# Transposed probabilities copied a pair at a time, out of two banks by one instruction

## The chip, the cores and the metric

The kernel runs on one core of one Trainium2 chip. The metric is the device time of one execution in microseconds (us), the median of three runs. A profiled execution gives the trace: which engine ran what, when, and what ended each idle stretch.

The engines by the names of the profile: PE multiplies matrices (PEld is its weight load), DVE is the vector engine, ACT the scalar engine, POOL the general one, SP issues transfers. Each runs its own instructions in order, and they wait for one another by semaphores. PE writes into PSUM, eight banks of 512 fp32 columns on 128 partitions; ACT and DVE read it.

## What is computed

Two encoder trunks with the same weights, one over 512 tokens (s = 0) and one over 1024 (s = 1), two layers each. A layer projects its input, runs three kinds of attention side by side, gates them, projects back and normalises:

```python
def encoder_layer(x, ...):
    h = x @ w_in
    (a_q, a_k, a_v, a_g, b_cq, b_ckv, b_kr, b_g, c_q, c_k, c_v, c_g) = jnp.split(h, split_at, axis=-1)
    oa = window_attn(a_q, a_k, a_v, sink, t5_table) * jax.nn.silu(a_g)       # 8 heads, +-128 tokens
    ob = mla(b_cq, b_ckv, b_kr, ...) * jax.nn.silu(b_g)                      # 4 heads, all tokens
    oc = neighborhood_attn(c_q, c_k, c_v, rpb) * jax.nn.silu(c_g)            # 4 heads, 2-D window
    o = jnp.concatenate([oa, ob, oc], axis=-1) @ w_out
    return layer_norm(DEEPNORM_ALPHA * x + o, ln_g, ln_b)
```

Each attention is scores, softmax, and probabilities times values.

## The kernel before

**Stages.** Within a layer, first s = 0 and then s = 1: input projections, attention A (windowed), C (neighbourhood), B (all positions), output projection, normalisation. PE takes most of its time for the projections (`products`, L564), which the change leaves alone.

**Units, pairs and halves.** Attention is cut into units of 128 queries by one head. A and C units see two or three tiles of 128 keys (256 or 384 columns); B units see all, four tiles for s = 0 and eight for s = 1. Two units that follow one another are a pair. The probabilities of a unit are transposed by PE in halves of at most four key tiles, so a B unit of s = 1 has two halves (hf 0 and 1) and every other unit one. Per layer there are, in pairs, 16 in A, 8 in C and 8 in B for s = 0, and 32, 16 and 16 for s = 1.

**One unit's way.** PE computes scores into PSUM (`score`). DVE reduces them to a bound and, in A and C, adds the bias on the way into `pAC` (`bound_scores`, L1027, L1038, L1044). ACT takes the exponential (`exp_unit`, L813 and L817). PE transposes the probabilities into bank 4 or bank 5 (`transpose_probs`, L661). One of ACT and DVE copies the bank into `pt_sb` (`pt_copy`, L824 on ACT and L1052 on DVE). PE multiplies by the values (`values`, L693), and after every second pair transposes the reciprocal sums (L699).

**Who copies.** `copied_by_act` numbers all halves and gives the even ones to ACT and the odd ones to DVE. Both units of a pair are transposed one behind the other into banks 4 and 5, so ACT copies the first unit's bank and DVE the second's, side by side.

**What sets the order.** PE's order is `pe_steps`. In A and C cycle j is: scores of pair j, transposes of pair j-1, values of pair j-2. In B cycle j is: scores of unit 2j, transposes of pair j-1, scores of unit 2j+1, for s = 1 the transposes of the second half, values of pair j-1. ACT and DVE walk over units: at step i, DVE does the bound of unit i, then its copy of unit i-2; every fourth step it adds `group_scale` (L1072), `group_rinv` (L1058) and `group_out` (L1078). ACT at step i does its copy of unit i-2, then the exponential of unit i. In B of s = 1, steps 2j and 2j+1 hold the copies of half 0 and half 1 of pair j-1.

**What PE waits for.** A transpose waits for the probabilities and for the copy of what stood in its bank two halves earlier; the values wait for the copies of their half. Both go through `wait_copied`. The copies go to four slots of `pt_sb`, so two pairs of halves are held at once.

Of the kernel before, what the change touches and what calls it, by code (L numbers as in the profile page):

```python
# [21 lines left out]
ACT = mybir.ActivationFunctionType  # L22
AX = mybir.AxisListType

P = 128
# [91 lines left out]
def units_of(phase, s):  # L117
    return {"A": a_units, "C": c_units, "B": b_units}[phase](s)
# [11 lines left out]
def halves_of(u, s):  # L130

    n = key_tiles(u, s)
    return [range(c, min(c + 4, n)) for c in range(0, n, 4)]
# [61 lines left out]
LAG_T, LAG_FIN = 2, 6  # L195
# [5 lines left out]
def encoder_kernel(nc, ins, y_out):  # L201
# [18 lines left out]
    with ctx:  # L220
# [128 lines left out]
        def halves(s, ph):  # L349
            return halves_in_order(ph, s)  # L350


        half_index = {}
# [4 lines left out]
            unit_index.update({(s, x): n % STAT_COLS for n, x in enumerate(x for ph in "ACB" for x in units_of(ph, s))})  # L358

        def copied_by_act(s, u, hf):  # L360
            return half_index[s, (u, hf)] % 2 == 0

        all_units = [(s, u) for s in range(2) for ph in "ACB" for u in units_of(ph, s)]
        all_groups = [(s, ph, g) for s in range(2) for ph in "ACB" for g in range(len(units_of(ph, s)) // 4)]
# [41 lines left out]

        probs_no = Numbered(all_units)
        score_no = probs_no
        pt_act_no = Numbered([(s, h) for s in range(2) for ph in "ACB" for h in halves(s, ph) if copied_by_act(s, *h)])
        pt_dve_no = Numbered([(s, h) for s in range(2) for ph in "ACB" for h in halves(s, ph) if not copied_by_act(s, *h)])  # L410
        group_no = Numbered(all_groups)
        xh_no = Numbered([("xT", s, t, i) for s in range(2) for t in range(NTILES[s]) for i in range(2)])
        split_no = Numbered([(s, u) for s in range(2) for u in UNITS])
# [40 lines left out]
        def wait_full(eng, key):  # L454
            b, n, _ = uses[key]
            eng.wait_ge(bank_full[b], n + 1)
            return bank[b]
# [97 lines left out]
        def _(pe):  # L555
# [87 lines left out]
                last.then_inc(full(("fill", s, ph)), 1)  # L643

            def wait_copied(s, half):
                if copied_by_act(s, *half):
                    pe.wait_ge(pt_act, pt_act_no[s, half])
                else:
                    pe.wait_ge(pt_dve, pt_dve_no[s, half])

            def transpose_probs(s, ph, j, hf):
                for i in (2 * j, 2 * j + 1):
# [22 lines left out]
            def values(s, ph, j):  # L675


                okey = ("O", s, ph, j // 2)
                b = uses[okey][0]
                if j % 2 == 0:  # L680
                    wait_free(pe, okey)
                    if j == 2 and ph in FILLERS:
                        wait_full(pe, ("fill", s, ph))
                pair = units_of(ph, s)[2 * j:2 * j + 2]
                nk = key_tiles(pair[0], s)
                cols = slice(P * (j % 2), P * (j % 2) + P)
                for hf, chunks in enumerate(halves_of(pair[0], s)):
                    for u in pair:
                        wait_copied(s, (u, hf))
                    for c in chunks:  # L690
                        for k, u in enumerate(pair):
                            slot = half_index[s, (u, hf)] % 4
                            nc.tensor.matmul(bank[b][64 * k:64 * k + 64, cols], value_tile(s, u, c),  # L693
                                             pt_sb[:, slot, (c % 4) * P:(c % 4 + 1) * P], start=(c == 0), stop=(c == nk - 1))
                if j % 2:
                    g = j // 2
                    pe.wait_ge(rinv_spread, group_no[s, ph, g])
                    for m in range(2):
                        last = nc.tensor.transpose(bank[b][:, 256 + P * m:256 + P * m + P], rinv_wide[:, P * m:P * m + P], ident[:, :])  # L699
                    last.then_inc(bank_full[b], 1)  # L700
# [62 lines left out]
        def _(act):  # L763
# [53 lines left out]
                    nc.scalar.activation(pAC[:, i % 3, 0:m], pAC[:, i % 3, 0:m], ACT.Exp, bias=nmax[:, j:j + 1],  # L817
                                         scale=-1.0, accum_out=psums[:, j:j + 1]).then_inc(probs_done, 1)

            def pt_copy(s, u, hf):  # L820
                if copied_by_act(s, u, hf):
                    ps = wait_full(act, ("PT", s, u, hf))
                    n = len(halves_of(u, s)[hf]) * P
                    nc.scalar.activation(pt_sb[:, half_index[s, (u, hf)] % 4, 0:n], ps[:, 0:n], ACT.Copy).then_inc(pt_act, 1)  # L824

            layer_ln = (ln_stat, ln_sqrt, ln_coef, ln_norm)

# [6 lines left out]
            with act.Fori(0, DEPTH) as layer:  # L834
# [16 lines left out]
                for s, NT in enumerate(NTILES):  # L851
# [50 lines left out]
                    for ph in "ACB":  # L902
# [26 lines left out]
                        for i in range(len(U) + LAG_T):  # L929
                            if 0 <= i - LAG_T < len(U):  # L930
                                if ph == "B" and s:
                                    for u in U[i // 2 * 2 - 2:i // 2 * 2]:
                                        pt_copy(s, u, i % 2)
                                else:
                                    pt_copy(s, U[i - LAG_T], 0)
                            if i < len(U):
                                exp_unit(s, i, U[i])
                    for g in range(2):
# [14 lines left out]
        def _(dve):  # L953
# [91 lines left out]
                                                   scale=1.0, scalar=3e38, op0=ALU.add, op1=ALU.min,  # L1045
                                                   accum_out=nmax[:, j:j + 1]).then_inc(score_done, 1)

            def pt_copy(s, u, hf):
                if not copied_by_act(s, u, hf):
                    ps = wait_full(dve, ("PT", s, u, hf))  # L1050
                    n = len(halves_of(u, s)[hf]) * P
                    nc.vector.tensor_copy(pt_sb[:, half_index[s, (u, hf)] % 4, 0:n], ps[:, 0:n]).then_inc(pt_dve, 1)  # L1052

            def group_rinv(s, ph, g):
                u = units_of(ph, s)[4 * g + 3]
# [31 lines left out]
            with dve.Fori(0, DEPTH) as layer:  # L1087
                for s, NT in enumerate(NTILES):
# [61 lines left out]
                    for ph in "ACB":  # L1150
# [31 lines left out]
                        for i in range(len(U) + LAG_FIN):  # L1182
                            if i < len(U):
                                bound_scores(s, i, U[i])
                            if 0 <= i - LAG_T < len(U):
                                if ph == "B" and s:
                                    for u in U[i // 2 * 2 - 2:i // 2 * 2]:
                                        pt_copy(s, u, i % 2)
                                else:
                                    pt_copy(s, U[i - LAG_T], 0)  # L1190
                            if i >= 5 and (i - 5) % 4 == 0 and i - 5 < len(U):
                                group_rinv(s, ph, (i - 5) // 4)
                            if i >= 8 and (i - 8) % 4 == 0 and i - 8 < len(U):
# [393 lines left out]
```

## Time and profile before

| | |
|---|---|
| three runs | 2022.31 us median (2020.79 to 2022.73) |
| the profiled execution | 2022.05 us, its span 2020.2 us |
| PE busy, share of the span | 1844.7 us, 91% |
| DVE busy | 961.1 us, 48% |
| ACT busy | 788.1 us, 39% |
| copies into `pt_sb` on ACT (L824) | 224, 113.2 us |
| copies into `pt_sb` on DVE (L1052) | 224, 127.2 us |
| PE's part of the chain that ended last | 85% |

The busy shares are means over stages with different limits. In the first layer the stages that copy are, in us from the span's start: A of s = 0 at 195 to 234, C at 234 to 252, B at 274 to 315; for s = 1, A at 640 to 720, C at 720 to 763, B at 808 to 917. The second layer repeats them.

In the rows a line of the timeline is: start in us, length in us, engine, line, operation, output and inputs, shapes, count, and in brackets the idle time before it with the event that ended it. A new instruction on DVE or ACT may start about 0.1 us before the one ahead of it is shown to end.

### The profile page before, as it was taken

How to read it: one execution, taken by the hardware profiler on the slowest of the kernel's cores; microseconds unless marked ns; L12 is line 12 of the kernel's file. 1: busy time of each engine (PE TensorE's matmuls, PEld its weight loads, DVE VectorE, ACT ScalarE, POOL GpSimd, SP SyncE). 2: the span in 40 equal slices, each digit the busy share in tenths (PEclk: the TensorE clock that was granted, in tenths of full speed). 3: DMA queues.
4: the chain of work that ended last, by engine and by line, in shares of the span. 5: the costliest groups of instructions: out<-in, count | busy, mean ns of one | idle time of the engine just before them, and what ended most of it. 6: DMA issues, size and time to landing. Idle time of an engine off the chain costs nothing.

```text
span 2020.2 us, 32850 instructions
## 1 busy us (share of the span) xinstructions
PE 1844.7 (91%) x12594; PEld 1491.3 (74%) x12594; DVE 961.1 (48%) x2226; ACT 788.1 (39%) x1651; POOL 423.8 (21%) x484
## 2 busy tenths in 40 slices
PE   1899978999999998999959999789999999989996
PEld 0697657889987665888948865588898866568796
DVE  7334744511423875554441466443124267555626
ACT  3323643322123665552222356332112256645512
POOL 4322211311110063001132213023010102600003
PEclk9899999999999999999979999999999999999998
DMA  7464305211124110005035450332112251000312
GB/s 256 134 198 127 95 1 199 86 55 47 53 73 118 40 60 0 1 1 188 32 122 157 138 157 12 141 100 67 59 43 59 68 136 34 27 1 2 136 53 84
DMA packets 149023, 169.76 MB, mean 84 GB/s; under 512 B 18384, under 2 KB 134736, under 8 KB 148352
## 3 DMA queue, kind: packets, MB, share of 16 engines
q1 hardware_dynamic: 146928, 161.24, 25.9%
q10 hardware_dynamic: 1504, 4.78, 0.6%
q8 instruction: 104, 1.70, 0.3%
q0 software_dynamic: 432, 1.57, 0.2%
q14 instruction: 55, 0.45, 0.1%
HBM read 145.49 MB, written 32.65 MB: 88 GB/s over the span
## 4 chain that ended last, share of the span: by engine, by line
PE 85%; DVE 8%; ACT 3%; issue 2%; POOL 1%; DMA 1%; SPq 0%; ACTq 0%; DVEq 0%; POOLq 0%
PE psum L564 62%; PE psum L693 8%; PE psum L661 7%; PE psum L635 5%; DVE nmax L1027 2%; PE psum L699 2%; DVE pt_sb L1052 1%; DVE gT L976 1%; DVE x_lo L1018 1%; ACT pAC L817 1%; DVE qB_lo L1179 0%; POOL w_lo L451 0%; DMA qkC<-ln_in_b 0%; PE psum L642 0%; PE psum L573 0%
## 5 line engine op out<-in xcount | busy, mean ns | idle before, releaser
L564 PE MATMUL psum<-w_hi,x_hi 128*128 128x256 f32 x1344 | 383.9, 286 | 21.7 <-DVE x_lo L1199 14.1
L564 PE MATMUL psum<-w_lo,x_hi 128*128 128x256 f32 x1344 | 383.1, 285 | 0.0
L564 PE MATMUL psum<-w_hi,x_lo 128*128 128x256 f32 x1344 | 382.8, 285 | 0.0
L564 PE MATMUL psum<-x_hi,w_hi 128*128 128x512 f32 x816 | 324.3, 397 | 10.7 <-DVE x_lo L1018 10.7
L564 PE MATMUL psum<-x_hi,w_lo 128*128 128x512 f32 x816 | 324.8, 398 | 0.0
L564 PE MATMUL psum<-x_lo,w_hi 128*128 128x512 f32 x816 | 324.1, 397 | 0.0
L451 POOL TENSOR_TENSOR w_lo<-w_stage,w_hi 128x1024 fp32r<-128x1024 f32 (+1 forms) x82 | 162.3, 1989 | 731.4 <-ACT w_hi L848 731.3
L451 DVE TENSOR_TENSOR w_lo<-w_stage,w_hi 128x1024 fp32r<-128x1024 f32 (+1 forms) x78 | 138.9, 1797 | 331.8 <-ACT w_hi L848 331.8
L564 PEld LDWEIGHTS psum<-w_hi,x_hi 128*128 128x128 f32 x1344 | 259.5, 193 | 23.4 <-issue 23.2
L564 PEld LDWEIGHTS psum<-w_lo,x_hi 128*128 128x128 f32 x1344 | 259.6, 193 | 0.2
L564 PEld LDWEIGHTS psum<-w_hi,x_lo 128*128 128x128 f32 x1344 | 259.6, 193 | 0.0
L848 ACT ACTIVATE w_hi<-w_stage 128x1024 fp32r<-128x1024 f32 (+1 forms) x160 | 129.0, 859 | 243.0 <-PE psum L564 194.0
L824 ACT ACTIVATE pt_sb<-psum 128x256 f32<-128x256 f32 (+2 forms) x224 | 113.2, 505 | 218.1 <-PE psum L661 216.8
L564 PEld LDWEIGHTS psum<-x_hi,w_hi 128*128 128x128 f32 x816 | 154.4, 189 | 48.2 <-issue 11.1
L564 PEld LDWEIGHTS psum<-x_lo,w_hi 128*128 128x128 f32 x816 | 154.5, 189 | 37.7
L564 PEld LDWEIGHTS psum<-x_hi,w_lo 128*128 128x128 f32 x816 | 154.3, 189 | 37.1
L1274 POOL COPY rinv_wide<-rinv 128x256 f32<-128x256 f32 x96 | 38.3, 399 | 662.1 <-DVE rinv L1058 662.1
L817 ACT ACTIVATE pAC<-pAC,nmax 128x385 f32<-128x385 f32 (+3 forms) x288 | 164.8, 574 | 22.3 <-DVE nmax L1044 12.2
L1027 DVE TENSOR_REDUCE nmax<-psum 128x1 f32<-128x1024 f32 (+1 forms) x96 | 100.5, 1047 | 142.7 <-PE psum L564 141.4
L661 PEld LDWEIGHTS psum<-ident,pAC 128*128 128x128 f32 x768 | 81.4, 141 | 72.8 <-ACT pAC L817 63.5
L1052 DVE COPY pt_sb<-psum 128x256 f32<-128x256 f32 (+2 forms) x224 | 127.2, 568 | 11.7 <-PE psum L661 11.6
L1038 DVE CUSTOM_DVE_ANT_0 pAC<-psum,biasA,nsink 128x384 f32<-128x384 f32 (+1 forms) x192 | 108.6, 568 | 46.2 <-PE psum L635 41.0
(146 smaller groups left out, 2680.0 us busy)
## 6 DMA issues: line engine op xcount, KB each, us to landing
w_stage<-w_in SPq DMA_DIRECT2D x48, 512.0 KB, 4.4
w_stage<-w_in SPq DMA_DIRECT2D x88, 256.0 KB, 3.2
toep<-rpb_tile SPq DMA_DIRECT2D x12, 1152.0 KB, 15.4
rpb_tile<-rpb_col SPq DMA_DIRECT2D x48, 192.0 KB
qA<-y SPq DMA_DIRECT2D x18, 512.0 KB, 5.2
hT<-y SPq DMA_DIRECT2D x18, 512.0 KB, 11.2
y<-hT SPq DMA_DIRECT2D x18, 512.0 KB, 2.6
w_stage<-w_out SPq DMA_DIRECT2D x32, 256.0 KB, 4.0
```

Of the source, the lines that this page charges most:

```text
L451: last = eng.tensor_tensor(lo, src, hi.bitcast(F32), ALU.subtract)
L564: last = nc.tensor.matmul(out, w, x, start=(n == 0), stop=(n == len(pairs) - 1))
L635: nc.tensor.matmul(ps[:, 0:n], w, x, start=True, stop=True).then_inc(full(("S", s, u, 0)), 1)
L661: last = nc.tensor.transpose(ps[:, (c % 4) * P:(c % 4 + 1) * P], src[:, c * P:(c + 1) * P], ident[:, :])
L693: nc.tensor.matmul(bank[b][64 * k:64 * k + 64, cols], value_tile(s, u, c), pt_sb[:, slot, (c % 4) * P:(c % 4 + 1) * P], start=(c == 0), st ...
L699: last = nc.tensor.transpose(bank[b][:, 256 + P * m:256 + P * m + P], rinv_wide[:, P * m:P * m + P], ident[:, :])
L817: nc.scalar.activation(pAC[:, i % 3, 0:m], pAC[:, i % 3, 0:m], ACT.Exp, bias=nmax[:, j:j + 1], scale=-1.0, accum_out=psums[:, j:j + 1]).th ...
L824: nc.scalar.activation(pt_sb[:, half_index[s, (u, hf)] % 4, 0:n], ps[:, 0:n], ACT.Copy).then_inc(pt_act, 1)
L848: last = nc.scalar.activation(hi, src, ACT.Copy)
L1027: nc.vector.tensor_reduce(nmax[:, j:j + 1], b_scores(s, i), AX.XY, ALU.min).then_inc(score_done, 1)
L1038: nc.vector.tensor_tensor_reduce(out=pAC[:, i % 3, 0:n], in0=ps[:, 0:n], in1=reversed_keys(biasA[:, t - 1, kv, :] if t else biasA0[:, kv, ...
L1052: nc.vector.tensor_copy(pt_sb[:, half_index[s, (u, hf)] % 4, 0:n], ps[:, 0:n]).then_inc(pt_dve, 1)
```

## The change

A pair of halves is copied by one instruction that reads banks 4 and 5 together and writes two neighbouring slots of `pt_sb`. One engine copies the whole pair: ACT the even pairs, DVE the odd ones. The semaphores `pt_act` and `pt_dve` count pairs instead of halves, and `wait_copied` waits for the pair that a half belongs to. In A, C and B of s = 0 both engines have the copy at odd steps only, on DVE behind the bound and on ACT ahead of the exponential; in B of s = 1 half 0 of every pair falls to ACT and half 1 to DVE.

```diff
         def copied_by_act(s, u, hf):
-            return half_index[s, (u, hf)] % 2 == 0
+            return half_index[s, (u, hf)] // 2 % 2 == 0
...
             def wait_copied(s, half):
-                if copied_by_act(s, *half):
-                    pe.wait_ge(pt_act, pt_act_no[s, half])
+                first = half_list[s][half_index[s, half] // 2 * 2]
+                if copied_by_act(s, *first):
+                    pe.wait_ge(pt_act, pt_act_no[s, first])
                 else:
-                    pe.wait_ge(pt_dve, pt_dve_no[s, half])
+                    pe.wait_ge(pt_dve, pt_dve_no[s, first])
...
                 for hf, chunks in enumerate(halves_of(pair[0], s)):
-                    for u in pair:
-                        wait_copied(s, (u, hf))
+                    wait_copied(s, (pair[0], hf))
...
-            def pt_copy(s, u, hf):
-                if not copied_by_act(s, u, hf):
-                    ps = wait_full(dve, ("PT", s, u, hf))
-                    n = len(halves_of(u, s)[hf]) * P
-                    nc.vector.tensor_copy(pt_sb[:, half_index[s, (u, hf)] % 4, 0:n], ps[:, 0:n]).then_inc(pt_dve, 1)
+            def pair_copy(s, ph, j, hf):
+                pair = units_of(ph, s)[2 * j:2 * j + 2]
+                if not copied_by_act(s, pair[0], hf):
+                    for u in pair:
+                        wait_full(dve, ("PT", s, u, hf))
+                    n = len(halves_of(pair[0], s)[hf]) * P
+                    slot = half_index[s, (pair[0], hf)] % 4
+                    nc.vector.tensor_copy(pt_sb[:, slot:slot + 2, 0:n], psum[:, 4:6, 0:n]).then_inc(pt_dve, 1)
...
                                 if ph == "B" and s:
-                                    for u in U[i // 2 * 2 - 2:i // 2 * 2]:
-                                        pt_copy(s, u, i % 2)
-                                else:
-                                    pt_copy(s, U[i - LAG_T], 0)
+                                    pair_copy(s, ph, i // 2 - 1, i % 2)
+                                elif i % 2:
+                                    pair_copy(s, ph, i // 2 - 1, 0)
```

ACT's `pt_copy` becomes a `pair_copy` in the same way, with `nc.scalar.activation(..., ACT.Copy)`.

DVE in attention B of s = 1, in the kernel before: the bound of a unit is `nmax<-psum`, a copy is `pt_sb<-psum`.

```order
L1027 TENSOR_REDUCE nmax<-psum 128x1
L1052 COPY pt_sb<-psum 128x512
L1027 TENSOR_REDUCE nmax<-psum 128x1
L1052 COPY pt_sb<-psum 128x512
L1027 TENSOR_REDUCE nmax<-psum 128x1
L1052 COPY pt_sb<-psum 128x512
L1072 TENSOR_TENSOR gT<-psum,gT 128x2x128
L1027 TENSOR_REDUCE nmax<-psum 128x1
L1052 COPY pt_sb<-psum 128x512
L1058 RECIPROCAL rinv<-psums 128x4
```

DVE at the same place in the changed kernel.

```order
L1030 TENSOR_REDUCE nmax<-psum 128x1 x2
L1058 COPY pt_sb<-psum 128x1024
L1030 TENSOR_REDUCE nmax<-psum 128x1
L1078 TENSOR_TENSOR gT<-psum,gT 128x2x128
L1030 TENSOR_REDUCE nmax<-psum 128x1
L1058 COPY pt_sb<-psum 128x1024
L1064 RECIPROCAL rinv<-psums 128x4
```

One copy of 1024 columns stands behind every second bound, where one of 512 stood behind each.

DVE in attention A of s = 1, before, the steps of two units with `group_scale` and `group_out` among them; a bound is the three rows that begin with `pAC,nmax<-psum`.

```order
L1038 ISA pAC,nmax<-psum,biasA,nsink 128x384
L1038 ISA nmax 128x1
L1041 COPY pAC<-nsink 128x1
L1072 TENSOR_TENSOR gT<-psum,gT 128x256
L1038 ISA pAC,nmax<-psum,biasA,nsink 128x384
L1038 ISA nmax 128x1
L1041 COPY pAC<-nsink 128x1
L1052 COPY pt_sb<-psum 128x384
L1058 RECIPROCAL rinv<-psums 128x4
L1078 TENSOR_TENSOR gT<-psum,gT 128x256
```

DVE at the same steps in the changed kernel.

```order
L1041 ISA pAC,nmax<-psum,biasA,nsink 128x384
L1041 ISA nmax 128x1
L1044 COPY pAC<-nsink 128x1
L1078 TENSOR_TENSOR gT<-psum,gT 128x256
L1041 ISA pAC,nmax<-psum,biasA,nsink 128x384
L1041 ISA nmax 128x1
L1044 COPY pAC<-nsink 128x1
L1058 COPY pt_sb<-psum 128x2x384
L1064 RECIPROCAL rinv<-psums 128x4
L1084 TENSOR_TENSOR gT<-psum,gT 128x256
```

The copy keeps its place between the second bound and the reciprocal, and now covers both banks; the next two bounds have no copy behind them, since ACT takes that pair.

## Rows read from the trace of the kernel before

**Rows 1.** The chain that ended last, by line: 640 to 662, then 823 to 834 us.

```profile
by line: PE psum L661 27.2%; PE psum L693 26.8%; PE psum L635 25.0%; PE psum L642 9.0%; ACT pAC L817 5.5%; PE psum L699 5.0%; ACT pt_sb L824 1.7%; issue 0.3%
...
by line: PE psum L564 35.7%; DVE nmax L1027 22.3%; PE psum L693 19.9%; DVE pt_sb L1052 11.1%; PE psum L661 8.0%; issue 3.8%; DVEq L456 0.4%
```

**Rows 2.** Windows: stretch, length, busy us per engine, PE clock, DMA share, GB/s.

```profile
640.00:719.60 79.60, 79.55 (x696) 51.17 (x696) 63.05 (x270) 53.37 (x160) 6.90 (x17) 1.00 0.33 90
...
808.00:917.30 109.30, 106.35 (x952) 88.01 (x950) 60.63 (x84) 55.03 (x92) 3.20 (x8) 1.00 0.07 24
...
281.00:311.70 30.70, 21.86 (x189) 17.08 (x187) 13.75 (x26) 12.26 (x30) 1.20 (x3) 1.00 0.05 13
```

**Rows 3.** Groups by shape, whole span: count, busy us, mean ns, idle before.

```profile
L1027 DVE TENSOR_REDUCE nmax<-psum 128x1 f32<-128x1024 f32 x64 | 78.4, 1224 | 99.4 <-PE psum L564 98.2
...
L1052 DVE COPY pt_sb<-psum 128x512 f32<-128x512 f32 x80 | 54.5, 681 | 9.5 <-PE psum L661 9.5
...
L1052 DVE COPY pt_sb<-psum 128x384 f32<-128x384 f32 x96 | 52.7, 549 | 1.1 <-PE psum L661 1.1
...
L824 ACT ACTIVATE pt_sb<-psum 128x512 f32<-128x512 f32 x80 | 47.8, 597 | 121.5 <-PE psum L661 121.5
...
L824 ACT ACTIVATE pt_sb<-psum 128x384 f32<-128x384 f32 x96 | 47.1, 490 | 65.8 <-PE psum L661 64.8
```

**Rows 4.** Timeline, B of s = 1: one cycle, then the last pair.

```profile
823.92 1.23 DVE L1027 TENSOR_REDUCE nmax<-psum 128x1 f32<-128x1024 f32 x1 [0.44 <-PE psum L564]
...
825.06 0.68 DVE L1052 COPY pt_sb<-psum 128x512 f32<-128x512 f32 x1
...
825.89 1.09 PE L693 MATMUL psum<-pt_sb,vB 128*64 128x128 f32 x16 [0.17 <-DVE pt_sb L1052]
...
913.58 0.69 DVE L1052 COPY pt_sb<-psum 128x512 f32<-128x512 f32 x1 [2.30 <-PE psum L661]
...
913.89 1.16 PE L661 MATMUL psum<-ident,pB 128*128 128x128 f32 x8 [0.34 <-ACT pt_sb L824]
...
915.09 0.69 DVE L1052 COPY pt_sb<-psum 128x512 f32<-128x512 f32 x1 [0.48 <-PE psum L661]
```

**Rows 5.** Timeline, B of s = 0: one cycle, an even pair.

```profile
287.18 0.69 DVE L1027 TENSOR_REDUCE nmax<-psum 128x1 f32<-128x512 f32 x1 [2.26 <-PE psum L564]
...
288.74 0.69 DVE L1027 TENSOR_REDUCE nmax<-psum 128x1 f32<-128x512 f32 x1 [0.87 <-PE psum L564]
289.35 0.68 DVE L1052 COPY pt_sb<-psum 128x512 f32<-128x512 f32 x1
289.47 0.69 ACT L813 ACTIVATE pB<-psum,nmax 128x512 f32<-128x512 f32 x1 [0.59 <-DVE nmax L1027]
...
290.18 1.09 PE L693 MATMUL psum<-pt_sb,vB 128*64 128x128 f32 x16 [1.47 <-DVE pt_sb L1052]
```

**Rows 6.** Timeline, A and C of s = 1: DVE's copy and PE's next transposes.

```profile
650.18 0.55 DVE L1052 COPY pt_sb<-psum 128x384 f32<-128x384 f32 x1
...
650.99 0.87 PE L661 MATMUL psum<-ident,pAC 128*128 128x128 f32 x6
...
655.46 0.55 DVE L1052 COPY pt_sb<-psum 128x384 f32<-128x384 f32 x1
...
656.06 0.88 PE L661 MATMUL psum<-ident,pAC 128*128 128x128 f32 x6
...
741.20 0.55 DVE L1052 COPY pt_sb<-psum 128x384 f32<-128x384 f32 x1
...
742.27 0.87 PE L661 MATMUL psum<-ident,pAC 128*128 128x128 f32 x6
```

**Rows 7.** Timeline, A of s = 0: DVE's copy and PE's next transposes.

```profile
220.13 0.54 DVE L1052 COPY pt_sb<-psum 128x384 f32<-128x384 f32 x1
...
220.52 1.04 PE L661 MATMUL psum<-ident,pAC 128*128 128x128 f32 x6
...
221.01 0.31 PEld L661 LDWEIGHTS psum<-ident,pAC 128*128 128x128 f32 x3 [0.18 <-ACT pAC L817]
```

More of the change, by code:

```diff
@@ L408, in encoder_kernel @@
         score_no = probs_no
-        pt_act_no = Numbered([(s, h) for s in range(2) for ph in "ACB" for h in halves(s, ph) if copied_by_act(s, *h)])
-        pt_dve_no = Numbered([(s, h) for s in range(2) for ph in "ACB" for h in halves(s, ph) if not copied_by_act(s, *h)])
+        pt_act_no = Numbered([(s, h) for s in range(2) for ph in "ACB" for h in halves(s, ph)[::2] if copied_by_act(s, *h)])
+        pt_dve_no = Numbered([(s, h) for s in range(2) for ph in "ACB" for h in halves(s, ph)[::2] if not copied_by_act(s, *h)])
         group_no = Numbered(all_groups)
@@ L818, in exp_unit @@
                                          scale=-1.0, accum_out=psums[:, j:j + 1]).then_inc(probs_done, 1)
-            def pt_copy(s, u, hf):
-                if copied_by_act(s, u, hf):
-                    ps = wait_full(act, ("PT", s, u, hf))
-                    n = len(halves_of(u, s)[hf]) * P
-                    nc.scalar.activation(pt_sb[:, half_index[s, (u, hf)] % 4, 0:n], ps[:, 0:n], ACT.Copy).then_inc(pt_act, 1)
+            def pair_copy(s, ph, j, hf):
+                pair = units_of(ph, s)[2 * j:2 * j + 2]
+                if copied_by_act(s, pair[0], hf):
+                    for u in pair:
+                        wait_full(act, ("PT", s, u, hf))
+                    n = len(halves_of(pair[0], s)[hf]) * P
+                    slot = half_index[s, (pair[0], hf)] % 4
+                    nc.scalar.activation(pt_sb[:, slot:slot + 2, 0:n], psum[:, 4:6, 0:n], ACT.Copy).then_inc(pt_act, 1)
             layer_ln = (ln_stat, ln_sqrt, ln_coef, ln_norm)
@@ L1046, in bound_scores, with pair_copy @@
                                                    accum_out=nmax[:, j:j + 1]).then_inc(score_done, 1)
-            def pt_copy(s, u, hf):
-                if not copied_by_act(s, u, hf):
-                    ps = wait_full(dve, ("PT", s, u, hf))
-                    n = len(halves_of(u, s)[hf]) * P
-                    nc.vector.tensor_copy(pt_sb[:, half_index[s, (u, hf)] % 4, 0:n], ps[:, 0:n]).then_inc(pt_dve, 1)
+            def pair_copy(s, ph, j, hf):
+                pair = units_of(ph, s)[2 * j:2 * j + 2]
+                if not copied_by_act(s, pair[0], hf):
+                    for u in pair:
+                        wait_full(dve, ("PT", s, u, hf))
+                    n = len(halves_of(pair[0], s)[hf]) * P
+                    slot = half_index[s, (pair[0], hf)] % 4
+                    nc.vector.tensor_copy(pt_sb[:, slot:slot + 2, 0:n], psum[:, 4:6, 0:n]).then_inc(pt_dve, 1)
             def group_rinv(s, ph, g):
@@ L1186, in _ @@
                                 if ph == "B" and s:
[L1187 to L1190, printed above, removed]
+                                    pair_copy(s, ph, i // 2 - 1, i % 2)
+                                elif i % 2:
+                                    pair_copy(s, ph, i // 2 - 1, 0)
                             if i >= 5 and (i - 5) % 4 == 0 and i - 5 < len(U):
```

## The prediction

> **What bounds the kernel now.** I read the chain of work that ended last first, cut to the stages that copy, since the change touches nothing else. In A of s = 1 it is PE's lines one after another: scores, transposes, values and reciprocal transposes make 93% of that stretch, and the 7% of ACT lie at the stage's start [rows 1]. PE is busy for 79.55 of 79.60 us there, DVE for 63.05 and ACT for 53.37 [rows 2]. So A is PE's own pace, and time that DVE or ACT saves is worth nothing unless PE waits for it. In B of s = 1 the same view is another picture: DVE's bound has 22.3% of the chain and DVE's copy 11.1% [rows 1]. The timeline shows how. The scores of the second unit end, DVE's bound starts at 823.92, DVE's copy follows at 825.06, and PE's second half of the values starts at 825.89 after 0.17 us of waiting for that copy [rows 4]. In B of s = 0 the wait is 1.47 us in each pair, on the same two DVE steps: bound at 288.74, copy at 289.35, values at 290.18 [rows 5]. What counts is therefore when the last copy of a pair ends, and not how much copying there is.
>
> **What a pair copy costs.** The trace has no copy out of two banks. It has copies of 384 and 512 columns: 549 and 681 ns on DVE, 490 and 597 ns on ACT [rows 3]. That is 132 and 107 ns for each 128 columns, with about 153 and 169 ns that do not depend on size. Carried on, 768 columns take 0.945 us on DVE and 0.811 on ACT, and 1024 columns 1.209 and 1.025. A reduction over two banks exists, 1024 columns in 1.224 us [rows 3], which speaks for DVE's figure. From below, two banks could be read at once, which would make it 0.68; from above, crossing into a second bank could cost the fixed part again, 0.15 more. I take the slope. From the end of a copy to the PE work that waits for it I take 0.15 us: 825.06 + 0.68 to 825.89 [rows 4].
>
> So one instruction replaces two, and saves 0.15 us of engine time for each pair. But the two ran side by side on two engines, and now one engine does both: the pair is ready 0.53 us later on DVE (1.209 for 0.681), or 0.40 with A's shapes (0.945 for 0.549). The page "Advanced Engine Details and Errata" of the Trainium skill, section "The Read-Write Bubble", advises large tiles and one instruction over several banks, since latency shows between instructions; by it the saved 0.15 us would be the whole effect. The rows agree that there is such a fixed part, and say that it lies on an engine that has time to spare. The page "Perfetto Trace Analysis" of the same skill, section "Optimizing Scalar/DVE Operations", grants grouping its gain only on a saturated engine, and otherwise advises splitting where the engine holds up another; this stage is of the second kind.
>
> **B of s = 1.** ACT's copy of half 0 takes 0.43 us longer than the one it had; the transposes of half 1 that wait for it may slip by a tenth or so, and that lies under the later wait. Half 1 is now all DVE's and stands behind the second unit's bound, as DVE's single copy did. It starts at 825.06 and ends 1.209 later, so the second half of the values starts at 826.42 in place of 825.89 [rows 4]: 0.53 us for each pair that has scores beside it. There are 15 such pairs a layer, 30 in all: **15.9 us**. The last pair has no scores to fill the time. ACT's pair copy starts when both units are transposed, at 913.58, and ends with the 0.15 at 914.76; PE's transposes of half 1, now at 913.89, wait for it, 0.87 more [rows 4]. They push DVE's copy from 915.09 to 915.96, and that takes 0.53 longer, part of which lies under the first half of the values: 1.3 us together, for two layers **2.6 us**.
>
> **B of s = 0.** There is a sign each way. Even pairs go to ACT, whose order is now exponential, pair copy, exponential. The bound starts at 287.18, the exponential follows it by 0.73 (288.74 to 289.47) and takes 0.69, the pair copy ends 1.025 + 0.15 later at 289.78, against 290.18 now [rows 5]: 0.40 gained, since this copy is no longer behind the second unit's bound. Odd pairs go to DVE behind that bound and lose 0.53. Four of each per layer: 0.5 us a layer, **1.0 us**.
>
> **A of s = 1.** DVE now has its pair copy in every second cycle, the one in which it also has `group_scale`, the reciprocal and `group_out`. PE's next transposes need bank 4 first, and the wait for it is now for the whole pair; before, that was ACT's early copy. DVE's copy starts at 650.18 and would end with the 0.15 at 651.27, where PE starts at 650.99: 0.28 lost. Where a pair of two key tiles lies next to it PE is sooner: copy from 655.46 to 656.56, PE at 656.06, 0.50 lost [rows 6]. In eight pairs (one head group over eight query tiles) there are two of the latter, one of the former and one, where the copied pair itself is of two tiles, with none: 1.28 us. Four head groups and two layers: **10.2 us**. Behind the pair copy the next bounds start up to 0.4 late. The exponentials that follow are due a whole cycle later, so I take nothing. In the other cycles ACT's pair copy stands ahead of the second exponential, 0.32 us longer than ACT's copy now. Worked through with the durations above, the transposes that wait for this exponential have 0.1 to 0.2 us left, so I take nothing; if all 72 ACT pairs of A and C lost the whole 0.32 it would be 23 us.
>
> **A of s = 0.** Every fourth pair loses: copy from 220.13, ready at 221.22, PE due at 220.52, 0.70 lost. A wait of 0.18 for the second unit's exponential stands there already [rows 7] and goes under, so 0.52 remains, four times a layer: **4.2 us**.
>
> **C.** The bound is shorter and the copy comes earlier against PE: ready at 742.30 for a start at 742.27 [rows 6], 0.03. POOL's bias rows hang on the reciprocal, which comes 0.40 later; I find them still in time. Ten such places a layer at 0.03 to 0.15: **1.5 us**.
>
> **The ends of A and C.** There the transposes of the last pair have no scores ahead of them and nothing but the previous values to cover them, and ACT's longer copy before the last exponential shows too. No row gives it. It lies between 0.28 (the ordinary stall) and 1.3 (the end of B); I take 0.65, for eight ends **5.2 us**.
>
> **Sum.** 15.9 + 2.6 + 1.0 + 10.2 + 4.2 + 1.5 + 5.2 = 40.6 us on the profiled execution's 2022.05 (0.26 below the median of the runs): **2063 us**, 2.0% slower. Projections, loads and output stages stand as they were, and everything after an attention stage waits for it, so I see no place that gives a stall back.
>
> **The rivals.** *Only B counts* (12%). The profile books PE's idle before the transposes of A to ACT's exponential, as at 221.01 [rows 7]. If PE waits for that anyway, the later copy hides in A, C and their ends, and 19.5 us remain: 2042. Against it is PE's busy time of 79.55 in 79.60 [rows 2].
>
> *The clock falls* (4%). PE's waits could bring it from 2.4 to 1.2 GHz in a stage. If B of s = 0 fell in both layers, its 21.9 us of PE work [rows 2] would double, 44 us more: 2107. Against it: in that stretch PE is busy for 21.86 of 30.70 us and the granted clock is 1.00 all the same [rows 2], and no stage becomes emptier than that.
>
> *DVE's time is what paces* (3%), the case on the faster side. Were the loop in A and C closed over DVE's queue, each of the 112 DVE pairs would give back 0.153 us: 17 us, 2005. It decides from the point where DVE has no idle time left; DVE has 63.05 of 79.60 [rows 2]. The skill's "Perfetto Trace Analysis" puts DVE's cost per instruction on PSUM at about 125 ns, by which the estimate would be 14 us and 2008; no run here shows that it is on PE's way.
>
> *Two banks are read at once* (2%). A pair copy would last as long as one bank's copy does. Then B of s = 1 and A lose little and the even pairs of B of s = 0 gain 0.8 each: about 2020, no change to speak of. Against it is the reduction, which takes 1.224 us for two banks.
>
> **How the numbers follow.** My forecast has 79%. Its own range is 2048 to 2080: below, the smaller ends and A's stalls in part; above, 0.15 more per pair copy at some 90 places (13 us) or a part of ACT's 23 us. To hold 8 in 10 the low end goes to 2040, which takes in the case of B alone: **2040 to 2080**. A measurement of this kernel tells changes of over 0.2% from none. Faster by that: 3%. Within: 2%. Slower: 95%.
>
> **What would show it.** In the profile after: 112 copies each on ACT and DVE, DVE's of 1024 columns near 1.21 us and of 2x384 near 0.95. PE idle of about 0.7 us before the second half of the values in B of s = 1, released by DVE's copy, and B of s = 1 about 9 us longer. PE idle of 0.3 to 0.7 before every second group of transposes in A, released by DVE's copy, and A of s = 1 some 5 to 6 us longer. In B of s = 0 waits that alternate, shorter after ACT's copy and longer after DVE's. It would be wrong if the pair copies came out shorter than the slope says, if A stayed at 79.6 us, or if idle time showed up before transposes and belonged to ACT's exponential.

## The result, and the profile after

| | before | after |
|---|---|---|
| median, us (runs) | 2022.52 (2020.79 to 2023.47) | 2057.77 (2052.62 to 2061.85) |
| ratio, 95% interval | | 1.0174 (1.0145 to 1.0203) |
| profiled execution, span | 2022.05, 2020.2 | 2054.34, 2052.5 |
| B of s = 1, layers 1 and 2 | 151.86, 152.66 | 159.94, 159.92 |
| B of s = 0 | 60.79, 59.23 | 61.03, 61.04 |
| A of s = 1 | 81.59, 81.58 | 86.55, 86.55 |
| A of s = 0 | 38.95, 38.96 | 41.71, 41.70 |
| C of s = 1 | 43.06, 43.07 | 44.25, 44.26 |
| C of s = 0 | 17.37, 17.36 | 18.29, 18.29 |

The kernel became 1.7% slower. A stage length runs from PE's first instruction of the stage, for B its own projections included, to the end of its last values. Together the stages of both layers are 37.0 us longer; the rest of the profiled execution is 4.8 us shorter, though the change touches nothing there. The clock, of which the last section tells, moves single stages by 1 to 4 us from one execution to another.

The page after, first its engines: all three that the change touches are busy for a smaller share, in a longer span.

```profile
PE 1851.2 (90%) x12594; PEld 1487.8 (72%) x12594; DVE 952.9 (46%) x2114; ACT 774.8 (38%) x1539; POOL 424.4 (21%) x484
```

First two groups of the kernel before, the values of B and the transposes of A and C, with count, busy us, mean ns and idle before:

```profile
L693 PE MATMUL psum<-pt_sb,vB 128*64 128x128 f32 x1280 | 87.3, 278 | 27.6 <-DVE pt_sb L1052 27.6
...
L661 PE MATMUL psum<-ident,pAC 128*128 128x128 f32 x768 | 119.1, 284 | 4.6 <-ACT pAC L817 4.0
```

The groups of the kernel after. L1058 and L828 are the pair copies on DVE and ACT, L694 the values, L663 the transposes.

```profile
L694 PE MATMUL psum<-pt_sb,vB 128*64 128x128 f32 x1280 | 87.9, 279 | 37.6 <-DVE pt_sb L1058 32.0 <-ACT pt_sb L828 5.5
...
L663 PE MATMUL psum<-ident,pAC 128*128 128x128 f32 x768 | 117.8, 282 | 18.2 <-DVE pt_sb L1058 11.4 <-ACT pAC L818 3.3 <-ACT pt_sb L828 2.6
...
L1058 DVE COPY pt_sb<-psum 128x1024 f32<-128x1024 f32 x40 | 48.6, 1216 | 12.9 <-PE psum L663 12.9
L1058 DVE COPY pt_sb<-psum 128x768 f32<-128x768 f32 x48 | 45.7, 951 | 2.0 <-PE psum L663 2.0
...
L828 ACT ACTIVATE pt_sb<-psum 128x1024 f32<-128x1024 f32 x40 | 41.0, 1024 | 110.2 <-PE psum L663 110.2
...
L828 ACT ACTIVATE pt_sb<-psum 128x768 f32<-128x768 f32 x48 | 38.0, 791 | 0.0
```

A copy out of two banks costs what the slope of [rows 3] said: 1.216 and 0.951 us on DVE, 1.024 and 0.791 on ACT. And PE now waits for DVE's copy in two places: ahead of the values of B for 32.0 us, with 5.5 for ACT's beside it, where it was 27.6 in all, and ahead of the transposes for 11.4, where there was no such wait. All of the 11.4 us lie in A.

The chain that ended last, by line, in 11 us of B of s = 1 (834 to 845 us), answers to the second row of [rows 1]: DVE's copy has gone from 11.1% to 22.3%, the bound ahead of it from 22.3% to 16.1%.

```profile
by line: PE psum L564 29.5%; DVE pt_sb L1058 22.3%; PE psum L694 17.9%; DVE nmax L1030 16.1%; PE psum L663 7.9%; issue 6.7%; DVEq L456 0.4%
```

The timeline of the same cycle, then the last pair of the stage, beside [rows 4]:

```profile
834.32 1.23 DVE L1030 TENSOR_REDUCE nmax<-psum 128x1 f32<-128x1024 f32 x1 [1.06 <-PE psum L564]
...
835.47 1.22 DVE L1058 COPY pt_sb<-psum 128x1024 f32<-128x1024 f32 x1
...
836.73 1.09 PE L694 MATMUL psum<-pt_sb,vB 128*64 128x128 f32 x16 [0.57 <-DVE pt_sb L1058]
...
929.89 1.02 ACT L828 ACTIVATE pt_sb<-psum 128x1024 f32<-128x1024 f32 x1 [2.16 <-PE psum L663]
931.06 1.06 PE L663 MATMUL psum<-ident,pB 128*128 128x128 f32 x8 [1.26 <-ACT pt_sb L828]
...
933.51 1.09 PE L694 MATMUL psum<-pt_sb,vB 128*64 128x128 f32 x16 [0.36 <-DVE pt_sb L1058]
```

From the start of the bound to the second half of the values it was 1.97 us (823.92 to 825.89); now it is 2.41. Every cycle grew by as much, 7.02 and 7.24 us to 7.47 and 7.67.

B of s = 0, an even pair and the odd one behind it, beside [rows 5]:

```profile
302.37 1.01 ACT L828 ACTIVATE pt_sb<-psum 128x1024 f32<-128x1024 f32 x1
...
303.53 1.09 PE L694 MATMUL psum<-pt_sb,vB 128*64 128x128 f32 x16 [1.04 <-ACT pt_sb L828]
...
307.73 1.22 DVE L1058 COPY pt_sb<-psum 128x1024 f32<-128x1024 f32 x1
...
309.00 1.09 PE L694 MATMUL psum<-pt_sb,vB 128*64 128x128 f32 x16 [1.92 <-DVE pt_sb L1058]
```

The wait of 1.47 us in every pair has become 1.04 and 1.92 in turn.

A of s = 0 and two places in A of s = 1, DVE's pair copy and the transposes that wait for it, beside [rows 7] and [rows 6]:

```profile
220.34 0.95 DVE L1058 COPY pt_sb<-psum 128x768 f32<-128x768 f32 x1
...
221.44 0.85 PE L663 MATMUL psum<-ident,pAC 128*128 128x128 f32 x6 [0.64 <-DVE pt_sb L1058]
...
653.49 0.95 DVE L1058 COPY pt_sb<-psum 128x768 f32<-128x768 f32 x1
...
654.59 0.85 PE L663 MATMUL psum<-ident,pAC 128*128 128x128 f32 x6 [0.21 <-DVE pt_sb L1058]
...
659.02 0.95 DVE L1058 COPY pt_sb<-psum 128x768 f32<-128x768 f32 x1
...
660.12 0.85 PE L663 MATMUL psum<-ident,pAC 128*128 128x128 f32 x6 [0.42 <-DVE pt_sb L1058]
```

### The profile page after: what moved, and what is told of

The parts are those of the page before. It is cut to its first block, busy times and chain, and to the rows that moved or that the text cites. A ratio compares the mean times of both kernels' runs of the same rounds, so it can differ in the third digit from the quotient of the medians.

```text
span 2052.5 us, 32718 instructions
## 1 busy us (share of the span) xinstructions
PE 1851.2 (90%) x12594; PEld 1487.8 (72%) x12594; DVE 952.9 (46%) x2114; ACT 774.8 (38%) x1539; POOL 424.4 (21%) x484
## 4 chain that ended last, share of the span: by engine, by line
PE 79%; DVE 12%; ACT 4%; issue 3%; POOL 1%; DMA 1%; SPq 0%; ACTq 0%; DVEq 0%; POOLq 0%
PE psum L564 60%; PE psum L694 6%; PE psum L663 6%; DVE pt_sb L1058 4%; PE psum L635 4%; PE psum L700 2%; DVE nmax L1030 2%; DVE gT L979 1%; DVE pAC L1041 1%; ACT pt_sb L828 1%; DVE x_lo L1021 1%; ACT pAC L818 0%; DVE qB_lo L1185 0%; POOL w_lo L451 0%; DMA qkC<-ln_in_b 0%
## 5 line engine op out<-in xcount | busy, mean ns | idle before, releaser
L663 PEld LDWEIGHTS psum<-ident,pAC 128*128 128x128 f32 x768 | 81.2, 141 | 89.5 <-ACT pAC L818 65.6
L828 ACT ACTIVATE pt_sb<-psum 128x512 f32<-128x512 f32 (+2 forms) x112 | 92.9, 830 | 112.7 <-PE psum L663 112.5
L663 PE MATMUL psum<-ident,pAC 128*128 128x128 f32 x768 | 117.8, 282 | 18.2 <-DVE pt_sb L1058 11.4
## 6 DMA issues: line engine op xcount, KB each, us to landing
hT<-y SPq DMA_DIRECT2D x18, 512.0 KB, 11.4
```

What stands on the lines that cost most here:

```text
L663: last = nc.tensor.transpose(ps[:, (c % 4) * P:(c % 4 + 1) * P], src[:, c * P:(c + 1) * P], ident[:, :])
L828: nc.scalar.activation(pt_sb[:, slot:slot + 2, 0:n], psum[:, 4:6, 0:n], ACT.Copy).then_inc(pt_act, 1)
```

## Experiments

**Is it the merged instruction, or that one engine does both banks?** The kernel after, with each pair as two one-bank instructions on the same engine:

```diff
-                    nc.vector.tensor_copy(pt_sb[:, slot:slot + 2, 0:n], psum[:, 4:6, 0:n]).then_inc(pt_dve, 1)
+                    for k in range(2):
+                        last = nc.vector.tensor_copy(pt_sb[:, slot + k, 0:n], psum[:, 4 + k, 0:n])
+                    last.then_inc(pt_dve, 1)
```

and the same on ACT.

> The changed kernel, but each pair is copied by two instructions of one bank each on the pair's engine, with the signal on the second; engines, order and waits are those of the change. Theory (one engine now does both banks, so the pair's last copy ends late): the two run one behind the other and end about 0.06 us later than the one instruction (0.60 + 0.68 for 1.22), so B of s = 1 stays at 160 to 163 us a layer (152 before), A of s = 1 at 86.5 to 88 (81.6 before), and the time at 2055 to 2066. Rival (it is the instruction over two banks that costs, by itself or by meeting PE in the other bank): the time falls back to 2022 to 2030.

Measured: 2068.29 us (2066.87 to 2070.49), 1.0241 (1.0224 to 1.0258), a little above what was expected. The merge is no loss; without it the kernel is slower still. Of the 10.5 us between the two, 3.1 are not the copies': they lie ahead of the first values of B of s = 1 in the first layer, in a stretch whose granted clock is in the last section. A of s = 1 is 87.37 and 87.38. The timeline shows two DVE copies in a row, and the values behind them:

```profile
843.28 1.28 DVE L1061 COPY pt_sb<-psum 128x512 f32<-128x512 f32 x2
...
844.62 1.09 PE L694 MATMUL psum<-pt_sb,vB 128*64 128x128 f32 x16 [0.58 <-DVE pt_sb L1061]
```

Two copies take 1.28 us and one of twice the size 1.22. A merge thus saves 0.06 and not the 0.153 of the slope, because the second copy starts before the first is shown to end: each alone lasts 0.68.

**Is it DVE?** The kernel after, with all pair copies on ACT:

```diff
-            return half_index[s, (u, hf)] // 2 % 2 == 0
+            return True
```

> The changed kernel with every pair copy on ACT; DVE copies none. Theory: what counts is when the pair's copy ends, and on ACT it is not behind DVE's bound. B of s = 1 then goes back to about 152 us a layer, B of s = 0 gains 0.44 us in all eight pairs of a layer and falls to 56 or 57, A of s = 1 is between (82.5 to 85), because the pair copy now stands ahead of the second exponential in every cycle; the time is 2015 to 2032. Rival (ACT's longer copy ahead of the exponential is what cost the time): it stands there twice as often, so the time rises over 2058, and A of s = 1 over 87.

Measured: 2029.79 us (2026.14 to 2031.6), 1.005 (1.0033 to 1.0067), as the theory expected. Of the 35 us, 28 are gone with DVE's share of the copies, though ACT now does them all.

```profile
L694 PE MATMUL psum<-pt_sb,vB 128*64 128x128 f32 x1280 | 87.5, 279 | 20.4 <-ACT pt_sb L828 17.5
...
L663 PE MATMUL psum<-ident,pAC 128*128 128x128 f32 x768 | 124.5, 285 | 7.6 <-ACT pAC L818 3.3 <-ACT pt_sb L828 2.9
```

The values wait for 20.4 us, against 37.6 after and 27.6 before. B of s = 0 gains 4.5 us a layer on the kernel before (56.12 and 54.76), A of s = 1 still costs 2.9 (84.50). B of s = 1 has its ordinary cycles back (7.07 and 7.23 to 7.26), but not its 152 us: it takes 153.37 and 155.48, 1.1 of it more at the last pair and, in the second layer, 1.4 more ahead of its first values.

**How much of it is B of s = 1?** The kernel before, with the pair copies in that stage alone:

```diff
+        def merged(s, ph):
+            return s == 1 and ph == "B"
...
-            return half_index[s, (u, hf)] % 2 == 0
+            n = half_index[s, (u, hf)]
+            return n // 2 % 2 == 0 if merged(s, u[0]) else n % 2 == 0
```

> The kernel before with one part of the change alone: pair copies in B of s = 1, half 0 on ACT and half 1 on DVE; A, C and B of s = 0 copy by halves as before. Theory: the stages lose independently of one another, so B of s = 1 goes to about 160 us a layer and all other stages stay, 2036 to 2041. Rival (a general slowing, of the clock or of DMA, that shows in this stage): this stage alone gives much less, under 2030, or other stages move too.

Measured: 2039.74 us (2039.26 to 2040.1), 1.0097 (1.008 to 1.0113). The cycles are 7.49 and 7.67, as in the kernel after, and A and C stay as before to 0.01 us. That is 18.7 us over the runs of before beside it, about half of the 35, and B of s = 1 alone brings it. Not all of it is the copies': the stage takes 162.94 and 160.65 us, 19.1 more than in the trace of before, of which cycles and last pair make 16.0, and 3.1 lie ahead of the first layer's first values, at a mean granted clock of 0.86 where the kernel before had 0.96.

**Does the place behind the bound decide in B?** The kernel before, with DVE's copy ahead of the bound at B's odd steps:

```diff
+                            late = ph == "B" and i % 2
-                            if i < len(U):
+                            if i < len(U) and not late:
...
+                            if i < len(U) and late:
+                                bound_scores(s, i, U[i])
```

> The kernel before, copies by halves, with one thing moved: at odd steps of B DVE does its copy ahead of the bound instead of behind it. Theory (PE's values wait for the last copy, and it is late because it stands behind the bound of scores that PE has only just done): B of s = 0 loses its 1.47 us wait nearly whole, about 1.3 us in each of eight pairs, 59 to 49 us a layer; B of s = 1 loses its 0.2 us and goes to about 149; the time is 1993 to 2003. Rival (the bound, now later, holds up the exponential and with it the next transposes): waits move from the values to the transposes and the time stays within 2018 to 2030 or rises.

Measured: 2001.19 us (2000.62 to 2002.69), 0.9908 (0.9892 to 0.9925). In B of s = 0 the timeline has copy, then bound, and a wait of 0.18 in place of 1.47 [rows 5]:

```profile
292.32 0.69 DVE L1052 COPY pt_sb<-psum 128x512 f32<-128x512 f32 x1 [0.18 <-PE psum L661]
...
293.02 0.69 DVE L1027 TENSOR_REDUCE nmax<-psum 128x1 f32<-128x512 f32 x1
293.16 1.09 PE L693 MATMUL psum<-pt_sb,vB 128*64 128x128 f32 x16 [0.18 <-DVE pt_sb L1052]
```

B of s = 0 falls to 51.62 and 50.51 us, which shows the place as the cause of the wait. B of s = 1 does not fall to the 149 us of the theory (152.33 and 151.61). Only its cycles without a reciprocal gain (6.69); the others grow to 7.49, since the reciprocal stayed behind the bound and PE now waits for what POOL makes of it:

```profile
825.10 0.17 DVE L1058 RECIPROCAL rinv<-psums 128x4 f32<-128x4 f32 x1
...
825.79 0.44 PE L699 MATMUL psum<-ident,rinv_wide 128*128 128x128 f32 x2 [0.49 <-POOL rinv_wide L1277]
```

**The same in the changed kernel,** with pair copy and reciprocal ahead of the bound at B's odd steps (the diff as above, with the reciprocal moved too):

> The changed kernel with one thing moved: at odd steps of B, DVE's pair copy and the reciprocal stand ahead of the bound instead of behind it. Theory: the pair copy is late in B because of the bound it stands behind, and a copy over two banks is not dear in itself. B of s = 0 falls from 61 to about 55.5 us a layer (only the DVE pairs gain, 1.3 each), B of s = 1 from 160 to about 155.5 (the copy is then bound by its own 1.22 us behind the transposes), A and C stay; 2034 to 2042. Rival (one engine for both banks is what costs, wherever its copy stands): B of s = 1 stays near 160 and the time at 2050 or more.

Measured: 2047.55 us (2045.47 to 2048.74), 1.0129 (1.0112 to 1.0146): better than after by 10 us, and short of what was expected. B of s = 0 came near the forecast (56.26, 56.15 for 55.5), B of s = 1 did not (159.55, 159.52 for 155.5): it stayed near 160, as the rival said.

```profile
831.80 1.09 PE L694 MATMUL psum<-pt_sb,vB 128*64 128x128 f32 x16
831.97 1.23 DVE L1058 COPY pt_sb<-psum 128x1024 f32<-128x1024 f32 x1 [1.98 <-PE psum L663]
833.12 1.22 DVE L1030 TENSOR_REDUCE nmax<-psum 128x1 f32<-128x1024 f32 x1
833.25 1.09 PE L694 MATMUL psum<-pt_sb,vB 128*64 128x128 f32 x16 [0.36 <-DVE pt_sb L1058]
...
924.09 0.66 PE L663 MATMUL psum<-ident,pB 128*128 128x128 f32 x4 [0.69 <-ACT pB L814]
```

Ahead of the bound the copy now starts as soon as the transposes end. But it takes 1.23 us, and the first half of the values covers 1.09 from 831.80 on, so 0.36 of idle time stays. In this stage one engine for both banks costs wherever its copy stands. The cycles are 0.2 us shorter than after (7.28 and 7.47). The bound is 1.2 us later, which is hidden in the cycles but not at the last pair: its exponential makes PE wait 0.69 and the end of the stage, from the last pair's transposes on, is 1.9 us longer (5.90 to 7.84).

**Do A and C lose by DVE's fuller cycle?** The kernel after, with the engines swapped between even and odd pairs in A and C:

```diff
-            return half_index[s, (u, hf)] // 2 % 2 == 0
+            return half_index[s, (u, hf)] // 2 % 2 == (u[0] != "B")
```

> The changed kernel with the engines swapped in A and C: even pairs to DVE, odd ones to ACT; B as in the change. DVE's pair copies then fall into the cycles in which it has no scaling and no reciprocal. Theory (in A and C the stall comes of a DVE cycle that holds two bounds, the scaling, a pair copy and the reciprocal): A of s = 1 falls from 86.5 to 82.5 to 84.5 us a layer, A of s = 0 from 41.7 to about 40, C by 0.5 to 1 in both; 2042 to 2052. Rival (a pair copy on one engine stalls A by its length alone): A of s = 1 stays at 86 or more and the time does not move.

Measured: 2049.95 us (2048.24 to 2053.5), 1.015 (1.0133 to 1.0167). The direction is the theory's, A of s = 1 (85.06) a little above its range.

```profile
L663 PE MATMUL psum<-ident,pAC 128*128 128x128 f32 x768 | 121.1, 284 | 11.1 <-ACT pAC L818 5.7 <-DVE pt_sb L1058 2.6 <-ACT pt_sb L828 1.7
```

The transposes' wait for DVE's copy falls from 11.4 to 2.6 us, while that for ACT's exponential rises from 3.3 to 5.7. In the cycle with the extra group work ACT's longer copy, which stands ahead of an exponential, costs 0.14 to 0.18 us where DVE's cost 0.28 and 0.50.

**Or is it the wait for the whole pair?** The kernel before, whose transposes wait for both copies of the pair two halves earlier:

```diff
-                        wait_copied(s, half_list[s][before])
+                        for b in range(before // 2 * 2, before // 2 * 2 + 2):
+                            wait_copied(s, half_list[s][b])
```

> The kernel before, with every copy where it was, but the transposes wait for both copies of the pair two halves earlier, as in the changed kernel. Theory (A loses because DVE does both banks' copies late in its fuller cycle, not because the wait covers the pair): DVE's copy of one bank from 650.18 ends with 0.15 at 650.88, before PE's 650.99, nothing lost; from 655.46 it ends with 0.15 at 656.16, 0.10 after 656.06. That is 1 to 2 us over both layers, and up to 0.1 for a second wait on one instruction at some 30 places: 2022 to 2027, A of s = 1 at 81.6 to 82.6 us. Rival (the wait for the whole pair is what costs in A and C): most of the 10 us of A of s = 1 and 5.5 of A of s = 0 come with it, about 2038, A of s = 1 at 86.

Measured: 2028.85 us (2027.55 to 2032.96), 1.0049 (1.0032 to 1.0067), above the theory's range and far from the rival's. A of s = 1 is 82.02 and 82.07, as the theory had it; A and C of both layers are 2.0 us longer together. Of the rest, 0.4 us a layer stand at the last pair of B of s = 1, whose cycles are as before; what is left lies at the starts of stages and between them, where nothing was changed. In A, the wait costs what DVE's single copy leaves of it; the 10 us come with the double one.

```profile
L662 PE MATMUL psum<-ident,pAC 128*128 128x128 f32 x768 | 115.9, 282 | 7.5 <-DVE pt_sb L1053 3.7 <-ACT pAC L818 3.3
```

**Why did B of s = 1 lose 0.44 us in a cycle and not 0.53?** The copy ends at 835.47 + 1.22 = 836.69 and the values start at 836.73, 0.05 later by the unrounded times (54 to 55 ns at all 40 places of B where the values wait for DVE). Before it was 0.15 (825.74 to 825.89). Before, the values' first instruction waited for two semaphores, ACT's and DVE's; after, for one. The kernel after, with the second half of the values waiting for the first half's copies as well, which ended long ago:

```diff
-                    wait_copied(s, (pair[0], hf))
+                    for h in range(hf + 1):
+                        wait_copied(s, (pair[0], h))
```

> The changed kernel with one wait added: the second half of the values in B of s = 1 also waits for half 0 of its pair, which ACT has long copied. Theory (the 0.15 us from the end of DVE's copy to PE's values in the kernel before, against 0.04 after, comes of the two waits on that instruction): the values start 0.15 after the copy again, the cycles of B of s = 1 grow from 7.47 and 7.67 to 7.58 and 7.78, and the stage from 160 to 161.7 us a layer; 2056 to 2066. Rival (the latency goes with the length of the copy): nothing moves.

Measured, in one run: 2060.9 us, and the cycles are 7.58 and 7.75 for 7.47 and 7.67, as the theory expected.

```profile
837.28 1.21 DVE L1059 COPY pt_sb<-psum 128x1024 f32<-128x1024 f32 x1
...
838.64 1.09 PE L695 MATMUL psum<-pt_sb,vB 128*64 128x128 f32 x16 [0.67 <-DVE pt_sb L1059]
```

The values start 0.15 after the copy (838.49 to 838.64): the second wait gives back the 0.09 that the merge had saved, and the cycles grow by 0.11 and 0.08. It is the same behind ACT. In B of s = 0 of the kernel with all copies on ACT, the even pairs, whose values also wait for a free output bank, start 0.14 after the copy, and the odd pairs, which wait for the copy alone, 0.05.

**Would pair copies in B pay on ACT?** The kernel before, with B's copies merged and all on ACT (`merged` true for B, `copied_by_act` true there):

> The kernel before with pair copies in B alone, all of them on ACT. Theory (B loses where DVE's pair copy stands behind the bound; the merge itself is harmless): B of s = 0 is 4.5 us a layer shorter, as it was with all copies of the kernel on ACT, B of s = 1 is 1 to 3 us a layer longer; A and C as before: 2014 to 2021. Rival (one copy for a pair costs in B on whatever engine, since nothing runs side by side any more): B of s = 1 at 160 us, 2036 or more.

Measured: 2019.84 us (2017.19 to 2023.04), 1.0 (0.999 to 1.0009). B of s = 0 gains 6.0 and 3.1 us (54.76, 56.11), B of s = 1 loses 4.7 and 3.9 (156.56, 156.59). Of the loss, 1.6 us a layer belong to the copies (0.5 over the cycles, 1.1 at the last pair); the rest stands ahead of the first values, where the mean granted clock was 0.86 in both layers and 0.96 and 0.93 in the kernel before. So there is no gain in all.

**A version that beats both.** From these, one copy for each bank and both engines side by side, as before, but DVE's copy and reciprocal ahead of the bound at B's odd steps:

> The kernel before, copies by halves, with DVE's copy and the reciprocal ahead of the bound at odd steps of B; the run with the copy alone moved left the reciprocal behind the bound, and its cycles with the transposes of the reciprocals (L699) took 7.49 us in B of s = 1 where they took 7.24 before. Theory (there PE waits for the reciprocal, by way of POOL): those cycles fall to about 6.9, B of s = 1 to 146 to 149 us a layer, B of s = 0 stays at 50 to 51.5, and the time is 1988 to 1996. Rival (those cycles wait for the later exponential instead): B of s = 1 stays at 152 and the time at 1999 to 2003.

Measured: 1994.72 us (1990.74 to 1995.87), 0.9867 (0.9851 to 0.9884), inside the expected range. B of s = 0 is 51.41 and 51.50, B of s = 1 148.49 and 148.29.

```profile
823.46 2.04 PE L693 MATMUL psum<-pt_sb,vB 128*64 128x128 f32 x32
823.57 0.69 DVE L1052 COPY pt_sb<-psum 128x512 f32<-128x512 f32 x1 [0.91 <-PE psum L661]
...
824.26 1.19 DVE L1027 TENSOR_REDUCE nmax<-psum 128x1 f32<-128x1024 f32 x1
```

A copy of one bank (0.69 us) fits under the first half of the values, and the two halves run on as one group of 32.

## Why the prediction was right, and where a term was off

The forecast of 2063 us was 5 above the median and 9 above the profiled execution. The mechanism is the one that was forecast: the pair's last copy ends later, and PE waits for it in B and in A. That the sum came so near is in part luck, as the terms show. For two layers:

| term | predicted, us | measured, us |
|---|---|---|
| B of s = 1, cycles and last pair | 15.9 + 2.6 | 13.4 + 2.6 |
| B of s = 0 | 1.0 | 2.1 |
| A of s = 1, with its ends | 10.2 + 1.3 | 9.9 |
| A of s = 0, with its ends | 4.2 + 1.3 | 5.5 |
| C, with its ends | 1.5 + 2.6 | 4.2 |

- **The price of a pair copy** held to 0.01 us on DVE and to 0.02 on ACT. The rivals that two banks are read at once, or that DVE's time paces, have nothing in the trace for them.
- **B of s = 1, cycles:** this term was mis-sized. The copy grew by 0.53, as said; the 0.15 from its end to PE, which I carried over, fell to 0.05, since the wait for a pair is one semaphore. That is 6.75 and 6.62 us over the 15 cycles of the two layers, for 7.95 each. The experiment with the second wait shows the 0.09. The two stages as a whole are 15.3 longer and not 16.0: up to its first values the stage is as long as before in the first layer and 0.7 us shorter in the second.
- **The last pair:** PE's wait for ACT's copy and then for DVE's makes 1.3 us a layer, as forecast from [rows 4].
- **B of s = 0:** the ordinary pairs changed by -0.43 and +0.43 (5.03 to 4.60 and 5.20 to 5.63) for -0.40 and +0.53. They cancel, so the 1.0 that the sum had from them did not come. The end of the stage, for which the sum had no term here, is 0.5 longer in each layer and makes the same 1.0: that is luck. The other 1.1 us lie at the stage's start and in its first pairs, which differ as much between the two layers of the kernel before (6.37 and 5.17 us from the first pair's transposes to the next).
- **A of s = 1:** the two stalls are the 0.28 and 0.50 of [rows 6], to 0.01: the times from one group of transposes to the next went from 2.45 and 2.24 to 2.73 and 2.74. Eight pairs take 1.21 more, for 1.28; the end of the stage takes 0.73 more, for 0.65. The count was one too high: of the eight stalls of 0.50 in a layer seven came, since the first head group has only one. That is why the stage grew by 4.96 and not by four times 1.21 with the end.
- **A of s = 0:** 0.70 less the wait that was there, 0.52 net, as [rows 7] gave it. But three such places came in a layer and not four, and the end of the stage took 1.0 for 0.65; the two errors cancel.
- **C and the ends:** about 0.03 in the ordinary cycles of s = 1, and 0.4 to 1.0 at each end of A and C. My 0.65 was a choice between 0.28 and 1.3, and right in the mean.
- **ACT's longer copy ahead of the second exponential** costs nothing in A and C, as taken: PE's wait for the exponential is 3.3 us in all (4.0 before). The 2.6 us that PE waits for ACT's pair copies there lie at 12 places at the starts and ends of stages. With the engines swapped it does cost, so the cover of 0.1 to 0.2 us was real and thin.
- **Only B counts** was the nearest rival. It falls: A and C make 19.7 of the 37.0 us, and PE waits there for DVE's copy above all.
- **The signs** came, smaller than said: A of s = 1 grew by 5.0 us (5 to 6 said), B of s = 1 by 8.1 and 7.3 (9 said), and PE's wait in its cycles is 0.57 (0.7 said).
- **What was wrong beside the sum:** "saves 0.15 us of engine time for each pair" holds against two copies on two engines, where each stands alone. Against two in a row it is 0.06. The page "Perfetto Trace Analysis" of the Trainium skill, section "Optimizing Scalar/DVE Operations", says that the last part of an instruction overlaps the next, and advises splitting work where an engine that is not saturated holds up another. The first experiment agrees with the overlap (1.28 us for two copies of 0.68). A split on one engine brought nothing there; that a split over two engines does is shown by the kernel before and the last version, each against its merged form (2022.52 for 2057.77 us, 1994.72 for 2047.55).
- **The rest of the execution**, which the sum left as it was, was 4.8 us shorter (1233.8 to 1229.0 us outside the attention stages). Without that the profiled execution would have come 4 us under the forecast and not 9. In the twelve profiled executions here, none of which changes that rest, it goes from 1228.9 to 1235.3, so the 4.8 lie within what it does by itself; what moves it stays open.

## What to carry to other kernels

Where two engines copy side by side and a consumer needs both parts, merging the parts on one engine delays the consumer by the difference between one copy and two, and here the saved fixed cost lay on an engine with time to spare; price the last arrival. Before merging, look at what the copy stands behind in its engine's queue: here moving it, with the reciprocal, ahead of the bound gave 1.3%, where the merge lost 1.7%. At a stage's last pair there is less work to cover a wait (1.3 us a layer here in B of s = 1), so price it apart.

## What was unexpected of the hardware

**Waits on one PE instruction.** From the end of a copy to the values it was 0.05 us with one semaphore to wait for and 0.15 with two, though the other had been reached long before. In A, where the transposes wait for more than one, it was 0.15 after too (654.44 to 654.59).

**The clock at a stage's start.** B of s = 1 begins with the same 134 matrix instructions (projections, transposes, first scores) in the kernel before and in the first experiment. The windows of that start (columns as in [rows 2]), first of the kernel before, then of the first experiment:

```profile
765.16:807.15 41.99, 36.91 (x134) 19.46 (x135) 22.05 (x42) 24.86 (x55) 13.90 (x48) 0.96 0.00 0
```

```profile
779.30:823.38 44.08, 39.71 (x134) 21.43 (x135) 22.14 (x42) 25.18 (x56) 13.96 (x48) 0.87 0.00 1
```

The mean granted clock is 0.96 in one and 0.87 in the other, and the stretch takes 2.1 us longer for equal work. In the kernel before, PE transposes the queries, stands idle for 1.45 us while DVE splits them, and the lower of the clock's two levels, 1.2 GHz and not 2.4, is granted from 800.5 to 803.9 us: there one score instruction starts every 0.43 us, later one every 0.23. In the experiment PE does the same work, and the lower level is granted from 811.6 to 825.3 us, from those transposes on and through all the first scores. Stages that differ by 1 to 4 us are therefore compared here by their cycles, and not by their whole length.
